# Two-layer fp32 decoder trunk on one core: the second layer's forget queries and keys made turned, in six blocks, behind the dilated chunk and the forget values

## The reference, cut to what matters

```python
def _mixer(x, w_in, b_f, w_pa, w_pb, w_pc, w_o):
    hcat = jnp.einsum('bsd,de->bse', x, w_in)
    ...
    qa, ka, va, fa, qb, kb, vb, qc, kc, vc, g = jnp.split(hcat, offsets, axis=-1)
    ya = _fox_attention(_heads(qa, 6), _heads(ka, 6), _heads(va, 6), fa + b_f)
    yb = _dilated_attention(_rope(_heads(qb, 12), pos), _rope(_heads(kb, 4), pos), _heads(vb, 4))
    yc = _moba_attention(_rope(_heads(qc, 6), pos), _rope(_heads(kc, 6), pos), _heads(vc, 6))
    ...
def reference(x, ...):
    x = _layer_norm(x, ln_in_g, ln_in_b)
    for l in range(2):
        x = _layer_norm(DN_ALPHA * x + _mixer(x, ...), ln1_g[l], ln1_b[l])
        x = _layer_norm(DN_ALPHA * x + _swiglu(x, ...), ln2_g[l], ln2_b[l])
```

## Time and profile before

| | |
|---|---|
| median of 3 runs | 829.08 us (828.97 to 829.12) |
| the profiled execution | 829.22 us, of which span 827.4 us |
| PE (matmul) busy | 816.9 us, 99% of the span |
| DVE / ACT busy | 536.0 us (65%) / 445.1 us (54%) |
| chain that ended last | PE 96%, DVE 2%, ACT 1% |
| mean granted TensorE clock | 0.998 |
| HBM read | 146.6 MB, 178 GB/s over the span |

### The profile page before, as it was taken

The page is one execution under the profiler, slowest core; times in us unless marked ns, Lnnn a source line. Parts: engine busy times, 40 slices in busy tenths (PEclk is TensorE's granted clock), DMA queues, the critical chain, the costliest instruction groups (busy, mean ns, idle before and its releaser), DMA issues.

```text
span 827.4 us, 11236 instructions
## 1 busy us (share of the span) xinstructions
PE 816.9 (99%) x4302; PEld 683.0 (83%) x4302; DVE 536.0 (65%) x783; ACT 445.1 (54%) x639; POOL 50.6 (6%) x91
## 2 busy tenths in 40 slices
PE   8999999999999999999999999999999999999996
PEld 5888888888888888888889788878888888888885
DVE  8665656475776767566767656564686767576764
ACT  4667767645455344434448677666454544434431
POOL 0022230000000000000000414100000000000000
PEclk9999999999999999999999999999999999999999
DMA  8854444566458565654437543437754675656511
GB/s 297 287 179 141 140 140 129 180 230 218 135 155 312 195 200 160 223 181 154 152 114 246 180 152 107 148 103 251 238 195 143 212 255 160 225 176 197 166 45 51
DMA packets 93501, 148.34 MB, mean 179 GB/s; under 512 B 3460, under 2 KB 54916, under 8 KB 93448
## 3 DMA queue, kind: packets, MB, share of 16 engines
q1 hardware_dynamic: 93296, 147.54, 54.4%
q10 hardware_dynamic: 152, 0.07, 0.0%
HBM read 146.56 MB, written 1.05 MB: 178 GB/s over the span
## 4 chain that ended last, share of the span: by engine, by line
PE 96%; DVE 2%; ACT 1%; issue 0%; DMA 0%; DVEq 0%
PE bank L1448 63%; PE bank L1474 16%; PE bank L1477 8%; PE bank L1428 2%; PE bank L1582 1%; PE bank L1491 1%; PE bank L1572 1%; PE bank L1560 1%; PE bank L1536 1%; PE bank L1501 1%; DVE w_lo L1147 1%; ACT prob_t_squares L1100 0%; DMA prob_t_squares<-in_norms 0%; DVE x L1376 0%; PE bank L1418 0%
## 5 line engine op out<-in xcount | busy, mean ns | idle before, releaser
L1147 DVE TENSOR_TENSOR w_lo<-raw,w_hi 128x2048 fp32r<-128x2048 f32 (+5 forms) x182 | 310.4, 1715 | 95.7 <-ACT w_hi L996 95.5
L1448 PE MATMUL bank<-w_hi,act_parts 128*128 128x512 f32 (+2 forms) x1120 | 349.8, 384 | 0.0
L996 ACT CAST w_hi<-raw 128x2048 fp32r<-128x2048 f32 (+3 forms) x140 | 253.9, 1814 | 101.3 <-PE bank L1477 57.9
L1448 PEld LDWEIGHTS bank<-w_hi,act_parts 128*128 128x128 f32 x1120 | 207.6, 188 | 38.4 <-issue 1.7
L1448 PE MATMUL bank<-w_lo,act_parts 128*128 128x512 f32 (+2 forms) x560 | 211.4, 378 | 0.0
L1474 PE MATMUL bank<-act_parts,w_hi 128*128 128x512 f32 x576 | 140.4, 391 | 0.0
L1474 PEld LDWEIGHTS bank<-act_parts,w_hi 128*128 128x128 f32 x576 | 105.7, 188 | 20.4
L1448 PEld LDWEIGHTS bank<-w_lo,act_parts 128*128 128x128 f32 x560 | 105.4, 188 | 16.9 <-issue 0.2
L1448 PE MATMUL bank<-w_hi,y_hi 128*128 128x512 f32 x240 | 94.9, 395 | 0.0
L1448 PE MATMUL bank<-w_lo,y_hi 128*128 128x512 f32 x240 | 93.6, 390 | 0.0
L1448 PE MATMUL bank<-w_hi,y_lo 128*128 128x512 f32 x240 | 93.5, 390 | 0.0
(11 more groups left out here) (137 smaller groups left out, 556.2 us busy)
## 6 DMA issues: line engine op xcount, KB each, us to landing
raw<-in_w_in SPq DMA_DIRECT2D x42, 1024.0 KB, 5.3
raw<-in_w_gate SPq DMA_DIRECT2D x44, 512.0 KB, 4.1
raw<-in_w_up SPq DMA_DIRECT2D x44, 512.0 KB, 5.2
raw<-in_w_down SPq DMA_DIRECT2D x22, 1024.0 KB, 5.0
raw<-in_w_o SPq DMA_DIRECT2D x8, 1024.0 KB, 5.2
raw<-in_w_in SPq DMA_DIRECT2D x8, 768.0 KB, 4.6
raw<-in_w_pa SPq DMA_DIRECT2D x4, 768.0 KB, 4.4
raw<-in_w_pc SPq DMA_DIRECT2D x4, 768.0 KB, 4.4
```

Of the source, the lines that this page charges most:

```text
L996: act.copy(weights(w_hi, i, HI_SLOTS), weights(raw, i, RAW_SLOTS)).then_inc(hi_done, 1)
L1147: dve.tensor_tensor(weights(w_lo, i, HI_SLOTS)[:, cols], weights(raw, i, RAW_SLOTS)[:, cols], weights(w_hi, i, HI_SLOTS)[:, cols].bitcast( ...
L1448: ins = pe.matmul(bank[use[0]][:, 0:width], a, w[:, k, c0:c0 + width], start=start and k == 0 and p == 0, stop=stop and k == nk - 1 and p ...
```

## The change

In layer 2 alone, chunks 0, 1 and 2 are replaced. The pieces come in the order chunk 3 (dilated), a new chunk `FORGET_VALUES` (all 384 forget values and the 6 gate columns), two half pieces of 512 columns of forget queries and keys, one piece of the other 256 columns with all 8 row tiles, then chunk 4 and on. Token tile 0 of chunk 3 and of the values runs first, as chunks 0 and 1 did. Then comes `forget`, and six blocks of 128 columns (0 to 2 queries, 3 to 5 keys) are made turned: per block 8 matmuls of 512 and 8 of 256 columns. DVE adds the two halves of the bank into `act_fns` (`fox_sum`), ACT casts this to `qk_hi`, and DVE writes `qk_lo` (`fox_lo`, one half block later in the list). `forget_sum` follows block 1, the first scores follow block 4, and the next attention step block 5. The stage copies and transposes of the forget branch are gone in layer 2.

```diff
@@ layer_pieces
+FORGET_VALUES = len(QKV)
+QKV.append((768, 390, [("v", 0, 0, 384), ("f", 0, 0, FOX_HEADS)]))
+FOX_BLOCKS = 6
+FOX_PIECE0_BLOCKS = 4
+FOX_GROUP = 3
...
+    if layer == 0:
+        chunks(range(1, FORGET_VALUES))
+    else:
+        chunks((3, FORGET_VALUES))
         for half in range(2):
-            piece(("qkv", c, half), [(rows(w["w_in"], 4 * half, 4, c0, width), 0, width)], 4, width)
+            piece(("fox", 0, half), [(rows(w["w_in"], 4 * half, 4, 0, NW), 0, NW)], 4, NW)
+        piece(("fox", 1), [(rows(w["w_in"], 0, KT, NW, 256), 0, 256)], KT, 256)
+        chunks(range(4, FORGET_VALUES))
@@ write_plan
-                stage_of[k]["qk"] = qk_last[b]
+                stage_of[k]["qk"] = ("fox", FOX_BLOCKS // 2 + p + 1) if layer and b == 0 else qk_last[b]
...
             for t in range(TT):
-                for c in range(2):
-                    use0 = bank(2 * c + t)
+                for n, c in enumerate((3, FORGET_VALUES)):
+                    use0 = bank(2 * n + t)
...
+            plan.append(("forget", layer, use0))
+            finish_lo()
+            lows = []
+            for j in range(FOX_BLOCKS):
+                use0 = bank(j % 4)
+                second = j >= FOX_PIECE0_BLOCKS
+                for half in range(2):
+                    i = at[("fox", 1)] if second else at[("fox", 0, half)]
+                    if not (second and half):
+                        prepare(i)
+                    plan.append(("fox_block", i, j, half, use0, [turned[t, half] for t in range(TT)]))
+                    if j in (FOX_PIECE0_BLOCKS - 1, FOX_BLOCKS - 1) and not (second and half == 0):
+                        release[i] = ("filled", use0) if half else ("used", count.next("used"))
+                        freed[0] += 1
+                    if half == 0 and lows:
+                        plan.append(("fox_lo", lows.pop()))
+                plan.append(("fox_sum", j, use0))
+                lows.append(j)
+                if j == 1:
+                    plan.append(("forget_sum", layer, aux_bank()))
+                if j >= FOX_PIECE0_BLOCKS:
+                    attend(True)
+                flush()
+            plan.append(("fox_lo", lows.pop()))
-        for c in range(2, len(QKV)):
+        for c in range(4 if layer else 2, FORGET_VALUES):
@@ scalar engine
+                elif kind == "fox_sum":
+                    _, j, (b, n) = step
+                    act.wait_ge(drained[b], n)
+                    act.copy(qk_hi[FOX_GROUP % 2][:, j, :], fox_block(j)).then_inc(fox_hi_done, 1)
@@ vector engine
+                elif kind == "fox_sum":
+                    _, j, (b, n) = step
+                    dve.wait_ge(filled[b], n)
+                    dve.tensor_reduce(fox_block(j), bank[b][:, :].rearrange("p (h n) -> p n h", h=2),
+                                      mybir.AxisListType.X, ALU.add).then_inc(drained[b], 1)
+                elif kind == "fox_lo":
+                    j = step[1]
+                    dve.wait_ge(fox_hi_done, j + 1)
+                    dve.tensor_tensor(qk_lo[FOX_GROUP % 2][:, j, :], fox_block(j),
+                                      qk_hi[FOX_GROUP % 2][:, j, :].bitcast(F32), ALU.subtract).then_inc(fox_lo_done, 1)
@@ tensor engine
+                        for long in (half == 0, half == 1):
+                            for k in range(4):
...
+                                if long:
+                                    ins = pe.matmul(out[:, :], wh[:, row, block], act_parts[:, at_k, :, :],
+                                                    start=first, stop=final)
+                                else:
+                                    ins = pe.matmul(out[:, 0:SEQ], wl[:, row, block], hi["act"][:, at_k, :],
+                                                    start=False, stop=False)
...
-                    pe.wait_ge(drained[qb], qn)
+                    pe.wait_ge(fox_lo_done if qb == "fox" else drained[qb], qn)
```

More of the change, by code:

```diff
@@ L88, in piece, with chunks @@
         order.append(name)
-    for c, (c0, width, _) in enumerate(QKV):
-        if layer == 0 and c == 0:
-            continue
+    def chunks(numbers):
+        for c in numbers:
+            c0, width, _ = QKV[c]
+            for half in range(2):
+                piece(("qkv", c, half), [(rows(w["w_in"], 4 * half, 4, c0, width), 0, width)], 4, width)
+    if layer == 0:
+        chunks(range(1, FORGET_VALUES))
+    else:
+        chunks((3, FORGET_VALUES))
         for half in range(2):
-            piece(("qkv", c, half), [(rows(w["w_in"], 4 * half, 4, c0, width), 0, width)], 4, width)
+            piece(("fox", 0, half), [(rows(w["w_in"], 4 * half, 4, 0, NW), 0, NW)], 4, NW)
+        piece(("fox", 1), [(rows(w["w_in"], 0, KT, NW, 256), 0, 256)], KT, 256)
+        chunks(range(4, FORGET_VALUES))
     for b, name in enumerate(("w_pa", "w_pb", "w_pc")):
@@ L475, in write_plan @@
             for t in range(TT):
-                for c in range(2):
-                    use0 = bank(2 * c + t)
+                for n, c in enumerate((3, FORGET_VALUES)):
+                    use0 = bank(2 * n + t)
                     for half in range(2):
                         if t == 0:
-                            second_norm(2 * c + half, at[("qkv", 0, 0)])
-                        qkv(c, t, (half,), use0, t == TT - 1, False)
+                            second_norm(2 * n + half, at[("qkv", 3, 0)])
+                        mm(at[("qkv", c, half)], t, ("act", ACT_SLOTS[half]),
+                           [(use0, 0, QKV[c][1], half == 0, half == 1)], t == TT - 1, turned[t, half],
+                           (use0,) if half else ())
+                    flush()
+                    qkv_done(c, t, use0)
                 if t == 0:
                     second_norm(4, 0)
-        for c in range(2, len(QKV)):
+            plan.append(("forget", layer, use0))
[4 more added lines that the diff above has]
+                second = j >= FOX_PIECE0_BLOCKS
+                for half in range(2):
+                    i = at[("fox", 1)] if second else at[("fox", 0, half)]
[13 more added lines that the diff above has]
+                    attend(True)
+                flush()
+            plan.append(("fox_lo", lows.pop()))
+        for c in range(4 if layer else 2, FORGET_VALUES):
             if c == 4:
@@ L699, in trunk, with fox_block @@
         tables = sb("tables", [P, TABLE_COLS])
+        def fox_block(j):
+            return act_fns[:, j * SEQ:(j + 1) * SEQ]
         def prob_t_of(u):
@@ L798, in trunk @@
         qk_hi_done = sem("qk_hi_done")
+        fox_hi_done = sem("fox_hi_done")
+        fox_lo_done = sem("fox_lo_done")
         cum_hi_done = sem("cum_hi_done")
@@ L1482, in _ @@
                         ins.then_inc(piece_used, 1)
+                elif kind == "fox_block":
+                    _, i, j, half, use, ready = step
+                    for b, n in ready:
+                        pe.wait_ge(drained[b], n)
+                    wait_lo(pe, i)
+                    _, nk, cols = pieces[i]
+                    wh = weights(w_hi, i, HI_SLOTS).rearrange("p (k n) -> p k n", k=nk)
+                    wl = weights(w_lo, i, HI_SLOTS).rearrange("p (k n) -> p k n", k=nk)
+                    at_j = j % FOX_PIECE0_BLOCKS
+                    block = slice(at_j * P, (at_j + 1) * P)
+                    if half == 0:
+                        take(use)
+                    out = bank[use[0]]
+                    for long in (half == 0, half == 1):
+                        for k in range(4):
+                            at_k = ACT_SLOTS[half][k]
+                            row = at_k if nk == KT else k
+                            first, final = half == 0 and k == 0, half == 1 and k == 3
+                            if long:
[4 more added lines that the diff above has]
+                                                start=False, stop=False)
+                    if half:
+                        ins.then_inc(filled[use[0]], 1)
+                    elif j == FOX_PIECE0_BLOCKS - 1:
+                        ins.then_inc(piece_used, 1)
                 elif kind == "turn":
```

## The result

The changed kernel takes **838.06 us** (median of 4 runs, 837.73 to 838.43), beside 829.10 for the kernel before on the same chip (828.97 to 829.25): a ratio of 1.0106 [1.0093, 1.0118], 9.0 us slower. The forecast was 835.4 with a range up to 837.6: right in its direction and mechanism, too small by 2.7 us and outside the range. The profiled execution took 838.16, its span is 836.0.

A forecast was written before the change was run, and what follows sets the result against it. PE, busy for 99% of the span, bounds the kernel. To the profiled 829.22 came +5.2 at chunk 4, -0.9 for transposes (net +4.3) and 2.0 for the clock: 835.5, less 0.14 for the median, 835.4 us; range 831.6 to 837.6.

The forecast's parts named there:

- PE's own work and its arrival: Layer 2 up to the first scores: block 0 starts at 437.3, PE is at the scores at 452.25.
- DVE's chain: DVE's queue from `logf_lo` to block 3's `fox_lo`: 15.6 us, ending at 458.1, so PE waits 6.0 us at the scores.
- Chunk 4: Start of chunk 4 after scores and block 5: 462.0 instead of 456.85, +5.2 us with the clock as it is.
- The clock: Clock falls to half in the wait before the first scores: 2.0 us lost, bounds 0 and 4.0.
- rival 1: At the first scores' wait the clock stays, the wait remains: 833.4 us, chance 0.30.
- rival 2: A smaller wait at the first scores, 2 to 4 us, with no fall: 829.5 to 831.5, chance 0.08.
- Behind chunk 4: After chunk 4's start: two groups of four transposes missing, -0.9 us, and nothing later gives the wait back.
- Rival 4: Fall costs up to 4.0, and a second wait follows at pair 1's scores or a softmax step: over 837.6, chance 0.06.
- The ends: Time around the profiled span: 1.8 us, taken as unchanged.
- Rival 3: DVE finishes block 3 before PE reaches the first scores, so PE's work decides: -1.6, 827.5 us, chance 0.06.

The follow-up runs named there:

- run 2: Changed kernel with 22 overwritten matmuls of 512 columns put ahead of PE's wait before the first forget scores: 836.17 us.
- run 5: Changed kernel with only the third weight split, the one right ahead of block 3's `fox_lo`, put behind the scores: 835.71 us.
- run 3: Changed kernel with the first forget scores behind block 5 instead of block 4, later attention steps in their old half steps: 834.51 us.
- run 8: The kernel of run 7 with block 4's sum put ahead of the held split on DVE: 829.92 us.
- run 9: The kernel before the change, with two more semaphores that nobody uses: 829.46 us.
- run 4: Changed kernel with the edits of run 1 and run 3 together: 835.83 us.
- run 6: The kernel of run 3 with 10 overwritten matmuls ahead of the wait at the scores: 832.45 us.
- run 7: Changed kernel with one split ahead in block 0, the others held until block 3's `fox_lo`, first scores behind block 5: 830.49 us.
- run 1: Changed kernel with the splits of the next three pieces put behind block 3's `fox_lo` on DVE: 836.27 us.

## Why the prediction was too small

**PE's own work and its arrival**: right. Block 0 was to start at 437.3 and starts at 437.25. PE was free at 452.76 instead of 452.25. Of this half microsecond some 0.2 is only that 452.76 is the end of a record, which runs past the start that a next matmul would have had; 0.3 is the one thing on this stretch that the forecast had considered and dismissed, POOL's rope of the dilated tile 1: it "would hold up its transposes at 440.1 only if it took over 5 us". It took 5.9:

```profile
434.40 2.61 POOL L990 TENSOR_TENSOR rope_cos<-stages,tables 128x128 f32<-128x128 f32 x1 [8.37 <-ACT stages L1068]
437.09 2.39 POOL L991 TENSOR_TENSOR rope_sin<-stages,tables 128x128 f32<-128x128 f32 x1
439.56 0.34 POOL L992 TENSOR_TENSOR stages<-rope_cos,rope_sin 128x64 f32<-128x64 f32 x1
439.98 0.32 POOL L993 TENSOR_TENSOR stages<-rope_cos,rope_sin 128x64 f32<-128x64 f32 x1
```

PE's transposes started at 440.36, as soon as this was done, where block 0 would have let them start at about 440.0. As the forecast said, a delay there was swallowed by the wait behind it: the wait is 5.4 and not 6.0, and ends at the same time.

**DVE's chain**: right to 0.1 us at its end, and with it the wait's end. **Chunk 4**: forecast at 462.0 with the clock as it was; measured 464.26 - 2.18 for the fall = 462.08.

**The clock**: forecast 2.0, measured 2.2 (run 2). That it would fall was the forecast, and rival 1, the clock stays, is out. That the two sizes lie so near each other is partly luck: the falls in mid-kernel cost 1.4, 2.2 and 2.7 us (runs 5, 2 and 3), and the 2.0 came from the kernel's start, where the length of the slow stretch varies too. In the changed kernel the first matmuls of 512 columns are 0.23 us apart from 6.01 on; in run 8 they are still 0.43 apart at 7.52. The 4.1 us without work that the forecast read from the end of the old run are no bound either. At the end of the profiled executions the clock falls 2.0 us (run 8), 3.5 (the changed kernel) and 5.3 (runs 3 and 9) behind PE's last matmul, by the windows view, and in the waits in mid-kernel 2.1 to 3.6 behind it. So rival 2, "2 to 4 us are left: 829.5 to 831.5, with no fall", was not safe in its last words; run 3 has just that wait, with a fall, and 834.5.

The Trainium skill's page TensorE: Matmul & The Clock Gate ("HAM oscillation") describes a kernel in which each wait for data of some 3 to 5 us brings the engine back cold. The waits of 3.5 and 4.0 us here agree with it, as does the longer one of 5.4; those of 2.5 and 2.6 are shorter than what it describes, and the clock fell in them as well.

**Behind chunk 4**: this is the main step that failed. The forecast had 0.9 for the missing transposes and "nothing later gives it back", and took all else as unchanged. Measured from chunk 4 to PE's end: 827.97 - 464.26 = 363.71, where 363.08 - 0.9 = 362.2 was due. The 1.5 are three waits, and the restarts behind them:

```profile
515.80 0.41 PE L1663 MATMUL bank<-tables,shared 128*128 128x128 f32 x2 [0.57 <-DVE y_lo L1305]
```

```profile
522.71 0.66 PE L1663 MATMUL bank<-tables,shared 128*128 128x128 f32 x4 [0.31 <-ACT shared L1127]
```

```profile
589.62 0.47 PE L1511 MATMUL bank<-w_hi,act_parts 128*128 128x512 f32 x1 [0.32 <-DVE act_fns L1318]
```

They sum to 1.2 of waiting. Rival 4 had a second wait "at the scores of pair 1 or a softmax step", and gave it 0.06, because pair 1 asks for its data 8 us later; that looked at the first pair alone. The cause is the change's `attend(True)` in block 4, a block ahead of chunk 4: it moves every later softmax step of the layer against the products, and their distances, which in the old order were just enough everywhere, no longer are in three places. Run 3 moves it back by a block and all three are gone, in runs 4, 6, 7 and 8 as well; in runs 1, 2 and 5, which leave it, all three stay.

**The ends**: 0.9 us more outside PE's path. This is the second step that failed: the forecast took the 1.8 around the span as unchanged, without a reason, and the tail too (run 9 has what is known of them). The range had room for a dearer fall, and none for either of these two.

So the sum is, in the forecast's terms: chunk 4 5.2 and the transposes -0.9, as forecast; the clock 2.2 (2.0); the three waits 1.5 (0); the ends 0.9 (0): 8.9, and the profiled executions differ by 838.16 - 829.22 = 8.94. Of the 2.7 that were missing more than half is the step behind chunk 4.

**Rival 3**, no wait at all: 827.5. Run 8 is this case, made by hand, and its profiled execution took 830.41, 2.9 more. Of these, 0.9 are the ends and 0.5 the remaining wait. 1.0 is that layer 2's products began at 417.43 in this execution, and at 416.39 in the old one. The delay is there from the start: layer 1's first scores begin at 51.77 instead of 50.68, behind the longer slow stretch at the kernel's start that is told above. In the other versions the products began between 416.3 and 416.9, so I don't charge it to the change. 0.4 is that chunk 4 came 40.1 behind them instead of 39.7, largely by POOL's rope. The last 0.1 is the old profiled execution beside the old median. So the gain in PE's own work is real, but it is no larger than what stands against it.

## What to carry to other kernels

When work for a full engine is replaced by work for one with slack, count the slack where the work is put: here DVE was busy for 65% of the span, and yet 12 rows of its queue stood between PE and its next operand. Three weight splits among them were put ahead to be early; putting them off is no cure, since the buffers that they free carry the delay to the next load, cast and softmax step, and what helped was to leave one ahead, hold the rest, and put the consumer behind one more block of products. Even that brought this kernel only back to its old time (run 8). A step of a software pipeline that moves by half a period moves all its successors, so look at every later place where the old distance was just enough, not only at the first.

A wait of some microseconds on a full TensorE costs more than its length when the clock falls in it: 1.4 to 2.7 us more in runs 2, 3 and 5. Taking the wait from 5.4 to 2.6 gave nothing of that back, while keeping the engine at useless work did.

## What was not expected of the hardware

- In the profiled executions the clock fell in waits of 2.5, 2.6, 3.5, 4.0 and 5.4 us (runs 1, 3, 5, 4 and the changed kernel). It stayed down for about 6.8 us in four of these cases, and for 3.4 in that of 3.5; these runs don't say what decides between the two.
- POOL's `rope_cos` and `rope_sin` operations took 2.61 and 2.39 us, where the same shape takes as little as 0.46 at other places of the layer. DVE ran two whole splits in that time, from 434.41 to 439.16, and they took 4.75 instead of 4.48:

```profile
434.41 4.75 DVE L1200 TENSOR_TENSOR w_lo<-raw,w_hi 128x2048 fp32r<-128x2048 f32 x2
```

  The first POOL operation ends at 437.01 and the second at 439.48, each within some 0.4 us behind the end of a split. The Trainium skill's page SBUF — State Buffer ("Who interferes with whom") has this rule: a DVE instruction with two inputs in SBUF contends with a GpSimd instruction that reads SBUF, and the ports that the two share are an exclusive lock. These rows agree with it, POOL's operations each lasting about a split (2.24) plus a little. The old kernel has one such pair too: a `rope_sin` of 2.39 at 456.16, with a split at 455.82. No run here separates the two engines.
